# Feed-forward rows of the ada product, shift by column halves and an earlier conv norm in a two-block transformer kernel

## The reference, cut to what matters

```python
ada = silu(c) @ w_ada + b_ada                     # (1, 6*1024), c is one row of 1024
sh_m, sc_m, g_m, sh_f, sc_f, g_f = split(ada, 6)
h = rmsnorm(x, norm_mix_g) * (1 + sc_m) + sh_m
x = x + g_m * hybrid_mixer(h)                     # w_in, latent and forget-gated attention, w_out
h = rmsnorm(x, norm_ffn_g) * (1 + sc_f) + sh_f
x = x + g_f * conv_ffn(h)                         # w_up, conv of width 3, silu gate, w_down
x = rmsnorm(x, norm_final_g)
# second block
hn = rms_norm(x, attn_norm_g)
xc, b_gate, c_gate, q, k, v = split(hn @ w_in_2)
y = b_gate * causal_depthwise_conv(c_gate * xc)   # then an rms norm by groups of 64, "conv norm"
mix = concat([conv_norm(y) * conv_out_g, diff_attention(q, k, v)])
x = x + mix @ w_out_2
x = x + moe(rms_norm(x))                          # 4 groups x 8 experts, top 2 of one group
```

## Time and profile before

| what | us |
|---|---|
| runs (3): median, lowest, highest | 1006.71, 999.34, 1006.77 |
| profiled execution, its own time | 1010.48 |
| its span, first to last instruction | 1008.7 |
| TensorE busy in the span | 957.3 (95%) |
| VectorE, ScalarE, GpSimd busy | 464.8, 378.6, 27.4 |
| weights and inputs read | 307.31 MB |

### The profile page before, as it was taken

One profiled execution on the slowest core, in us unless ns is written; L12 is line 12 of the kernel. 1 busy time (PEld: TensorE's weight loads), 2 busy tenths in 40 slices (PEclk: granted clock), 3 DMA queues, 4 the chain that ended last, 5 costly groups with the idle time before them and its releaser, 6 DMA issues.

```text
span 1008.7 us, 15018 instructions
## 1 busy us (share of the span) xinstructions
PE 957.3 (95%) x6185; PEld 665.4 (66%) x6185; DVE 464.8 (46%) x858; ACT 378.6 (38%) x718; POOL 27.4 (3%) x60
## 2 busy tenths in 40 slices
PE   6899999998999999999989899999999999998987
PEld 3798777898999999988988434343434343332433
DVE  2797756576787468667874411212121112110113
ACT  2465546555666356454662512121212111110211
POOL 1000000000000000002121000000000000000000
PEclk9999999998999999999999999999999999999999
DMA  9968833443754554534666699999999999999996
GB/s 387 400 258 301 331 140 142 202 178 115 274 197 167 177 199 168 199 136 167 269 233 251 265 430 428 427 427 428 428 428 426 428 429 427 427 427 429 429 426 267
DMA packets 23397, 309.34 MB, mean 307 GB/s; under 512 B 2592, under 2 KB 3104, under 8 KB 4000
## 3 DMA queue, kind: packets, MB, share of 16 engines
q1 hardware_dynamic: 23184, 307.32, 74.5%
q10 hardware_dynamic: 144, 1.05, 0.3%
HBM read 307.31 MB, written 1.05 MB: 306 GB/s over the span
## 4 chain that ended last, share of the span: by engine, by line
PE 78%; DMA 14%; DVE 5%; ACT 2%; issue 1%; POOL 0%; DVEq 0%; SPq 0%
PE ps L998 75%; DMA work<-experts 4%; DMA ring<-experts 4%; DMA slot<-experts 4%; DVE wl L1640 1%; DMA ring<-dense 1%; DMA early<-dense 1%; PE ps L1567 1%; PE ps L1196 1%; ACT wh L579 0%; PE ps L1509 0%; ACT hH L804 0%; PE ps L1161 0%; DVE xT L2067 0%; ACT wb L593 0%
## 5 line engine op out<-in xcount | busy, mean ns | idle before, releaser
L998 PE MATMUL ps<-hH,wh 128*128 128x256 f32 x704 | 201.0, 285 | 4.0 <-DVE hL L1664 1.9
L1640 DVE TENSOR_TENSOR wl<-ring,wh 128x1024 fp32r<-128x1024 f32 (+1 forms) x136 | 163.9, 1215 | 81.9 <-ACT wh L579 81.6
L998 PE MATMUL ps<-hL,wh 128*128 128x256 f32 x704 | 198.3, 282 | 0.0
L998 PE MATMUL ps<-hH,wl 128*128 128x256 f32 x704 | 198.2, 282 | 0.0
L579 ACT ACTIVATE wh<-ring 128x1024 fp32r<-128x1024 f32 (+1 forms) x136 | 140.6, 1043 | 121.5 <-PE ps L998 95.3
L998 PEld LDWEIGHTS ps<-hH,wh 128*128 128x128 f32 x704 | 133.9, 190 | 6.1 <-issue 3.7
L998 PEld LDWEIGHTS ps<-hH,wl 128*128 128x128 f32 x704 | 135.6, 193 | 0.0
L998 PEld LDWEIGHTS ps<-hL,wh 128*128 128x128 f32 x704 | 133.8, 190 | 0.0
L2336 DVE SCALAR_TENSOR_TENSOR wc<-wc,w_slot,ps 128x512 f32<-128x512 f32 x16 | 12.0, 748 | 220.9 <-PE ps L998 220.9
L998 PE MATMUL ps<-aH,wh 128*128 128x256 f32 x304 | 86.6, 285 | 5.9 <-DVE wb L2192 2.7
L998 PE MATMUL ps<-aL,wh 128*128 128x256 f32 x304 | 85.7, 282 | 0.0
(11 more groups left out here) (349 smaller groups left out, 1415.6 us busy)
## 6 DMA issues: line engine op xcount, KB each, us to landing
ring<-dense SPq DMA_DIRECT2D x39, 2048.0 KB, 8.5
ring<-experts SPq DMA_DIRECT2D x28, 2048.0 KB, 27.9
slot<-experts SPq DMA_DIRECT2D x28, 2048.0 KB, 28.9
work<-experts SPq DMA_DIRECT2D x20, 2048.0 KB, 28.3
early<-experts SPq DMA_DIRECT2D x10, 2048.0 KB, 26.6
wb<-experts SPq DMA_DIRECT2D x9, 2048.0 KB, 25.3
early<-dense SPq DMA_DIRECT2D x4, 2048.0 KB, 8.7
ring<-dense SPq DMA_DIRECT2D x4, 1024.0 KB, 4.7
```

Of the source, the lines that this page charges most:

```text
L998: return nc.tensor.matmul(o_, l, r, start=start, stop=stop, skip_group_check=True)
L1640: V.tensor_tensor(wl[:, c % CHUNKS, 0:n], src, wh[:, c % CHUNKS, 0:n].bitcast(F32), ALU.subtract)\
```

## The change

1. Shift by column halves: the shift's first item is columns 0 to 511 for all 8 blocks of rows; cq is loaded next; columns 512 to 1023 follow in two items. TensorE multiplies the second half between chunks 1 and 2 of cq. All ada items now use four strips (`ada_cols`), with a quarter of their columns on each; scale items 256 columns, shift items 128.
2. Of third 2, SC_F is now two items (behind g0 and g1; multiplied behind scores(0) and behind gate chunk 3), and G_F two items loaded behind wo1 and multiplied around `norm_spread` ahead of up0; G_F is transposed behind up1 and added behind after_up(0).
3. The conv norm: VectorE multiplies with b_gate ahead of mean_o2(2), ScalarE squares ahead of o2_out(2), VectorE takes the conv means ahead of the last split of w2o_attn, and TensorE spreads the rstd ahead of chunk 3 of w2o_attn.

```diff
--- dense_items
-    for nm, c0, k0, kn, slot in (("scale0", D, 0, 4, None), ("scale1", D, 4, 4, None), ("shift0", 0, 0, 4, 4),
-                                 ("shift1", 0, 4, 2, 5), ("shift2", 0, 6, 2, TAIL)):
-        item(f"ada_{nm}", kn, D, [("w_ada", k0, c0, D)], 0, None, slot)
+    for nm, c0, n, k0, kn, slot in (("scale0", D, D, 0, 4, None), ("scale1", D, D, 4, 4, None), ("shift0", 0, 512, 0, 8, 4)):
+        item(f"ada_{nm}", kn, n, [("w_ada", k0, c0, n)], 0, None, slot)
     in_item("cq", 0)
+    for nm, k0, slot in (("shift1", 0, 5), ("shift2", 4, TAIL)):
+        item(f"ada_{nm}", 4, 512, [("w_ada", k0, 512, 512)], 0, None, slot)
...
         in_item(f"g{i}", acc)
-        ada_item(2, i)
+        if i < 2:
+            item(f"ada_scale_f{i}", 4, D, [("w_ada", 4 * i, 4 * D, D)], 0)
...
         half_item("wo", j, "w_out", KD, 512, 2 - 2 * j)
+    for i in range(2):
+        item(f"ada_gate_f{i}", 4, D, [("w_ada", 4 * i, 5 * D, D)], 0)
--- SyncE
                 if it["name"] == "up4":
                     sp.wait_ge(S("chunk_low"), max(a["c1"] for a in items if a["slot"] == EARLY))
+                    sp.wait_ge(S("ada_used"), max(a["ada"] for a in items if a["slot"] == EARLY))
--- ScalarE
-            for i in range(4):
-                split("cq", i, i + 1)
-                if i == 0:
-                    act.wait_ge(S("ada_cols"), 1)
-                norm_high(0, adaT[:, SH_M:SH_M + KD], 2 * i, 2 * i + 2)
+            act.wait_ge(S("ada_cols"), 1)
+            norm_high(0, adaT[:, SH_M:SH_M + KD], 0, 4)
+            split("cq", 0, 3)
+            act.wait_ge(S("ada_cols"), 2)
+            norm_high(0, adaT[:, SH_M:SH_M + KD], 4, 6)
+            split("cq", 3)
+            norm_high(0, adaT[:, SH_M:SH_M + KD], 6, 8)
...
             high_o2(1)
+            act.wait_ge(S("cy_ready"), 2)
+            nc.scalar.activation(csq, cy, ACT.Square).then_inc(S("cv_sq"), 1)
             o2_out(2)
             squares_o2(3)
             split("w2o_attn", 2, 3)
-            act.wait_ge(S("cy_ready"), 2)
-            nc.scalar.activation(csq, cy, ACT.Square).then_inc(S("cv_sq"), 1)
             high_o2(2)
--- TensorE
+            def ada_cols(name, c0):
                 it = IT[f"ada_{name}"]
                 pe.wait_ge(S(f"slot{it['slot']}_loaded"), it["loaded"])
                 w = slot_view(it)
                 for kk in range(it["kn"]):
                     k = it["srcs"][0][1] + kk
+                    n = it["n"] // 4
+                    for q in range(4):
+                        ins = mm(ps[32 * q:32 * q + 1, 7, c0:c0 + n], cact[:, k:k + 1], w[:, kk, n * q:n * q + n],
+                                 k == 0, k == KD - 1)
                 ins.then_inc(S("ada_used"), 1)
+            def turn_cols(i, c0, n):
+                pe.wait_ge(S("ada_row"), i)
+                for c in range(c0, c0 + n, P):
+                    ins = nc.tensor.transpose(ps[:, 6, c:c + P], ada_row[:, c:c + P], ident[:])
                 ins.then_inc(S("ada_turned"), 1)
...
-            ada_half("scale0", 0)
+            ada_cols("scale0", 0)
             norm_totals(0, 5)
-            ada_half("scale1", 0)
+            ada_cols("scale1", 0)
             norm_spread("norm_rstd", 1, rstd, 4)
-            turn_half(0)
-            for i in range(3):
-                ada_half(f"shift{i}", 2)
-            turn_half(1)
-
-            linear("cq", hH, hL, True, ready=("norm_in", [IN_BASE[0] + k + 1 for k in range(KD)]))
+            turn_cols(1, 0, 256)
+            ada_cols("shift0", 256)
+            turn_cols(2, 256, 128)
+
+            h_in = ("norm_in", [IN_BASE[0] + k + 1 for k in range(KD)])
+            chunk("cq", 0, hH, hL, True, ready=h_in)
+            chunk("cq", 1, hH, hL, True, ready=h_in)
+            ada_cols("shift1", 384)
+            ada_cols("shift2", 384)
+            turn_cols(3, 384, 128)
+            chunk("cq", 2, hH, hL, True, ready=h_in)
+            chunk("cq", 3, hH, hL, True, ready=h_in)
...
-                if i % 4 == 3:
-                    ada_part(2, 1 + i // 4)
+                if i == 3:
+                    ada_cols("scale_f1", 0)
...
             scores(0)
-            ada_part(2, 0)
+            ada_cols("scale_f0", 0)
...
             linear("om0", aH, aL, False)
-            ada_turn(3)
+            turn_cols(4, 0, 256)
...
             norm_totals(1, 4, 4, KD)
+            ada_cols("gate_f0", 256)
             norm_spread("norm_rstd", 2, rstd, 5)
+            ada_cols("gate_f1", 256)
...
+                if j == 1:
+                    turn_cols(5, 256, 256)
...
             chunk("w2o_attn", 2, aH[:, 4:8], aL[:, 4:8], False, 0, True, False, o_in)
-            chunk("w2o_attn", 3, aH[:, 4:8], aL[:, 4:8], False, 0, True, False, o_in)
             pe.wait_ge(S("cv_rstd"), 1)
...
             ins.then_inc(S("cv_bc"), 1)
+            chunk("w2o_attn", 3, aH[:, 4:8], aL[:, 4:8], False, 0, True, False, o_in)
--- VectorE
+            def cols_row(c0, n, name):
+                dve.wait_ge(S("ada_used"), IT[name]["ada"])
+                V.tensor_copy(ada_row[:, c0:c0 + n], ps[:, 7, c0:c0 + n]).then_inc(S("ada_row"), 1)
+            def cols_out(i, c0, n, name, at):
+                cols_row(c0, n, name)
+                return cols_turned(i, c0, n, at)
...
+            scaled(0, 4)
+            cols_out(2, 256, 128, "ada_shift0", SH_M).then_inc(S("ada_cols"), 1)
+            dve.wait_ge(S("ada_cols"), 1)
+            scaled(4, KD)
+            shifted_low(0, 4)
+            split("cq", 0, 2)
+            cols_out(3, 384, 128, "ada_shift2", SH_M + 4).then_inc(S("ada_cols"), 1)
+            dve.wait_ge(S("ada_cols"), 2)
+            split("cq", 2, 3)
+            shifted_low(4, 6)
+            split("cq", 3)
+            shifted_low(6, KD)
...
             taps(2)
-            mean_o2(2)
-            split("w2o_attn", 1, 2)
-            low_o2(1)
-            scale_o2(2)
             done("bg")
...
+            mean_o2(2)
+            split("w2o_attn", 1, 2)
+            low_o2(1)
+            scale_o2(2)
             mean_o2(3)
             split("w2o_attn", 2, 3)
             low_o2(2)
             scale_o2(3)
+            dve.wait_ge(S("cv_sum"), 1)
+            mean_sq_of(ms, ps[:, 6, :], 8, D_CONV // 8, "cv_ms")
             split("w2o_attn", 3)
             low_o2(3)
-            dve.wait_ge(S("cv_sum"), 1)
-            mean_sq_of(ms, ps[:, 6, :], 8, D_CONV // 8, "cv_ms")
```

79 lines of the change are left out of this document (22 added, 57 removed).

## The result

| what | us |
|---|---|
| changed kernel, 20 runs: median, lowest, highest | 1009.82, 1003.91, 1014.9 |
| kernel before, 20 runs beside it | 1004.04, 999.34, 1006.77 |
| ratio after to before, 95% interval | 1.005, 1.0031 to 1.007 |
| profiled execution after: its time, span | 1010.92, 1009.2 |

The forecast was 1002.3 in a range up to 1008.5; 1009.82 lies above it. So the change gains nothing: the first measurement has it 0.3 to 0.7% slower, the intervals of the other two hold 1, and the gain of 4.4 us that was forecast isn't there. The ratios compare fast executions only, so two slow ones of the kernel before (1017.71 and 1016.77, beside e9 to e11) are left out, and they are not the quotients of the medians.

What follows compares the result with a forecast made beforehand. The expert stream's start was taken to set the end. Start +1.0, attention -1.3, norm -0.5 and conv norm -3.6 gave -4.4 us: 1006.1 for the profiled execution, 1002.3 for the median, range 994.5 to 1008.5.

Steps and rivals of the forecast that it cites:

- What bounds the kernel: Whole kernel: the end is the start of the expert stream plus a constant; dense-part gains before 572.64 count one for one.
- rival D: Whole kernel: the end does not follow the start of the experts, 1006.7 us; chance 0.05.
- Price of the ada items: Ada multiplications: 1.7 us per 16 matmuls of 256 columns, 2.3 us per 32 of 128 columns.
- the lower bound: Shift pieces of 128 columns: 1.7 us per 32 matmuls, priced by their columns alone.
- Rival A: Shift: narrow pieces cost 4.0 us per half, start +5.4, total +1.3, 1008.0 us; chance 0.1.
- its two lesser terms: Start: a second half-clock stretch behind the second hand-over; attention: the hole ahead of om0 costs 1.6 us.
- Start: Scale, shift, cq: cq begins near 29.2, but the second hand-over gives nearly all back; +1.0 us, ends -1.0 and +5.4.
- Attention: Gate chunks 7 and 11: 1.8 gained behind 7, about one chance in three of 1.6 lost before om0; -1.3 us.
- The item whose removal "gains nothing": Ada item behind gate chunk 11: it covered a path running beside it, so removal leaves a hole of nearly 3 us.
- Norm: Norm before feed-forward: 3.4 us of gate_f multiplying costs 0.3, a clock staying up gives 1.5 back; -0.5 us.
- Conv norm: Second mixer's conv norm: two holes and a half-clock stretch close, short waits remain; -3.6 us, ends -4.4 and -1.5.
- Rival C: Conv norm: the move only exchanges waits, conv -1.5, total -2.3, 1004.4 us; chance 0.2.

Runs made afterwards that it cites:

- the other two: Second and third measurements of the unchanged changed kernel against the kernel before, on two different chips: ratios 1.0024 and 0.9994.
- e9: Changed kernel plus a third transpose behind up1 (the first done twice): 1005.55 us, ratio 0.9973 to the kernel before.
- e11: Kernel before with four strips, whole shift ahead of cq, change's scale_f, gate_f behind gate chunk 11 and norm spread, conv-norm edit: 998.26 us, ratio 0.9927.
- e1: Kernel before with only the conv-norm edit: 1004.3 us, ratio 0.9987.
- e10: Changed kernel, all shift products plus unread ones ahead of cq, gate_f behind gate chunk 11 and norm spread, third transpose behind up1: 1000.66 us, ratio 0.9931.
- e14: Changed kernel unchanged, measured a third time against the kernel before: 1006.55 us, ratio 0.9994.
- e6: Changed kernel with unread one-row products filling holes ahead of cq's chunks 0 and 2 and om0: 1005.64 us, ratio 0.9983 to the kernel before.
- e7: Same kernel as e11, measured earlier against the kernel before: 1001.58 us, ratio 0.9957.
- e15: Changed kernel plus a third transpose behind up1, measured again: 1006.22 us, ratio 0.9995 to the kernel before.
- e2: Kernel before with only the four-strip scale and shift, the shift by column halves around cq's first chunks: 1007.23 us, ratio 1.0004.
- e8: Kernel before with two one-column matmuls behind each of up0 to up10 and dn0 to dn2: 1016.89 us, ratio 1.0116.

## Why the prediction was wrong

**What bounds the kernel: right.** The end follows the experts' start; rival D is refuted by the constant 454.6 to 456.2.

**Price of the ada items: right, with the lower bound.** 32 matmuls of 128 columns took 1.93 us where I took 2.3. Rival A's total of +1.3 is near what the stages give below, but its mechanism, pieces at 4.0 us, is refuted; its two lesser terms, the second stretch at half clock and the price of the hole ahead of om0, came true. The rule of the Trainium skill (TensorEngine Tiling (Array Packing), Instruction Overhead), about 60 cycles per matmul, would as an addition have made it 3.3; this trace disagrees with that reading, for four strips of 128 columns take the time of their columns.

**Start: +1.0 forecast.** The early cq is real (30.59 instead of 33.80; 29.2 was forecast), and so is the second hand-over of 2.5 us. In its own comparison my sum is off by 3.0 (47.76 instead of 44.8), half of it because scale0 and scale1 took 3.6 and 3.4 us, not 1.7 each, and the rest by the second stretch at half clock, which I had named as possible and not counted. Scale0 is slow at a granted clock of 1.00, and e1 had the same with two strips (5.55 us instead of 3.60), so this is no price of the strips: behind the wait for the first weights TensorE is sometimes slower, by up to nearly half, without the record of the clock saying so. The Trainium skill (TensorE: Matmul & The Clock Gate, Seeing it yourself) warns that the clock's events in a trace were seen to be unreliable; 3.59 against 1.91 us at a recorded 1.00 fits that. Against the mean of six profiles of the old start the loss is 1.5, near the forecast; but the scatter is larger than that, so this nearness is partly luck, and I had taken a lucky trace for the kernel.

**Attention: -1.3 forecast, the step that failed.** The 1.8 behind gate chunk 7 came (42.78 to about 40.97 in the kernels with part 2; 41.13 in e10). The hole of 2.91 us ahead of om0 came as I had said, and I gave it one chance in three of 1.6 us, so 0.5 in the sum. Both the chance and the price were too low: it cost 2.9 us in five of six profiles. In the sixth (e14) om0 took 9.46 behind the same hole; its first matmul, and the window of om0 at full clock:

```profile
192.63 0.39 PE L1002 MATMUL ps<-aH,wh 128*128 128x256 f32 x1 [2.91 <-DVE aL L1911]
```

```profile
192.60:198.00 5.40, 5.37 (x47) 5.37 (x48) 1.47 (x2) 1.06 (x1) 0.00 (x0) 1.00 0.90 322
```

So the length of the hole alone doesn't decide it, and what does stays open. The item whose removal "gains nothing" was mostly worth 2.9 us where it stood: it kept the clock up. e6 and e7 show it from both sides, one with unread products in the hole and one with the item back in it. The Trainium skill (TensorE: Matmul & The Clock Gate, HAM oscillation — how this bites in real kernels) says that a wait between groups of matmuls lets the clock fall, so that the next group begins at half rate; it speaks of waits longer than this hole. Here 2.91 us were enough in five of six profiles. The stage with g1 is 0.8 longer in the mean of the five profiles of the change (e9 and e15 among them). It takes 31.84 us without a stretch at half clock (e2, e9, e11), 33.4 to 33.5 with one (the kernel before and five others of its order), and 34.7 with two (e14 and e15, at 120 and 137). In the other two profiles of the change it has one, at 138, and 34.8 to 35.0 us, for g1's load took 11.1 to 11.3 us instead of 8.8 to 9.5; what makes that load late wasn't found.

**Norm: -0.5 forecast, -0.3 measured** (18.76 in the mean of five profiles of the change, 19.09 in seven without part 2), though not as I had it: gate_f0 ran at half clock in three of five (the stage then took 19.25 to 19.66), and in the two others the stage took 17.6.

**Conv norm: -3.6 forecast, -3.2 measured.** Rival C is refuted. The power behind the conv means took 3.81 us where I took 2.90, and is waited for by 1.33 instead of 0.5.

**Sum.** Stage by stage, in means and without the column "long": start +1.5, to g0 -0.2, g1 +0.8, g2 and g3 -1.8, om0 +2.4 (2.9 in five of six), om1 to wo1 +0.1, norm -0.3, q2 +0.8 (no edit is near; the table's scatter) and conv norm -3.2, together +0.1, against the -4.4 of the forecast. That fits the third measurement (-0.4 us in the median) and the second within its interval; the first, +5.8, it doesn't explain. The step that failed, the clock behind the hole ahead of om0, is thus some 2 of these 4.5 us, and the rest is spread over g1, q2, the start and the two norms. For the first measurement the granted clocks of the single runs say something more: the changed kernel's mean was 0.982 in the first and second measurement (20 and 12 runs) and 0.985 in the third (12 runs). The difference is worth up to 2.3 us, an estimate from these means and 1009 us that takes TensorE as busy all the time, and the changed kernel's mean time fell from 1009.50 to 1006.64. So more half clock can be most of what the changed kernel lost there. The kernel before was also 3.1 us faster in the mean in the first measurement than in the third (1003.90, 1007.05), with no clock on record; why both came together stays open.

**The reference point.** I went from one profiled execution to a median of three runs. Medians of the kernel before lay between 1004.04 and 1007.44 in the six measurements since. The spread has named causes now: the pace (6.5 us), the start (5.6), each stretch at half clock (1.5 to 3). My range took in the costs of the edits, and of the kernel's own scatter only "some".

## What to carry to other kernels

Work in a hole ahead of a dense stretch is not free to remove: count what the clock gives back before moving it, and put movable work (here the ada items) into the hole that is next to dense work, not into one that is short already. Where a trace has two paces or a start that varies, compare stages over several profiles before believing a difference of a few microseconds, and never judge a change of under 1% by times from separate measurements: medians of the kernel before lay 2.0 us apart even in two on one chip (1004.99 and 1006.98). When a stage is made earlier, look at the loads: here cq's weights at 31 us and ada10's at 44 set the next limit, in that order.

## What the runs showed that was not expected

- Unread products in a hole made the stage behind it shorter: twelve records, 2.75 us of filling in a hole of 2.9, save the 2.8 us that om0 otherwise loses at 1.2 GHz (e6).
- The same stream of matmuls runs at 10.88 or 11.31 us per 96 with the clock at 1.00; in these profiles the pace changes only at interruptions, with period three where two one-column matmuls follow each matrix (e8).
- The first products with weights take 3.60 or 5.39 to 5.87 us (two strips, three profiles each way), 1.91 or 3.2 to 3.6 (four strips, four profiles and seven), at a granted clock recorded as 1.00. In the changed kernel cq ends at 46.6 with the one (e14, e15) and at 47.8 to 48.2 with the other.
